# Two weight buffers moved to other start addresses in a TensorE-bound float32r kernel

## The reference

```
first block, 2 layers:
  mod = silu(c) @ w_mod + b_mod                      # shifts, scales, gates
  p = (rms_norm(x) * (1 + scale) + shift) @ w_in
  mix = [attention, fourier, conv, pool](p) @ w_out
  x = x + gate1 * mix
  x = x + gate2 * ((silu(xn @ w_a) * (xn @ w_g)) @ w_ffn_out)
second block, 2 layers:
  layer 0: retention and a short convolution, gated, @ w_out
  layer 1: low-rank (latent) causal attention, gated, @ w_out
  h = h + rms_norm(y) * post_norm
```

## Time and profile before

| | |
|---|---|
| median of 3 runs | 2270.41 us (2269.43 to 2270.57) |
| time of the profiled execution | 2271.93 us |
| its span from first to last instruction | 2269.8 us |
| TensorE matmul busy | 2203.6 us, 97% |
| TensorE weight load busy | 1776.2 us, 78% |
| VectorE busy | 1176.1 us, 52% |
| ScalarE busy | 732.7 us, 32% |
| GpSimd busy | 633.6 us, 28% |
| mean granted TensorE clock | 0.986 |

### The profile page before, as it was taken

The page is one execution under the profiler, slowest core; times in us unless marked ns, Lnnn a source line. Parts: engine busy times, 40 slices in busy tenths (PEclk is TensorE's granted clock), DMA queues, the critical chain, the costliest instruction groups (busy, mean ns, idle before and its releaser), DMA issues.

```text
span 2269.8 us, 26814 instructions
## 1 busy us (share of the span) xinstructions
PE 2203.6 (97%) x11148; PEld 1776.2 (78%) x11148; DVE 1176.1 (52%) x1533; ACT 732.7 (32%) x1101; POOL 633.6 (28%) x272
## 2 busy tenths in 40 slices
PE   8998899999999999999999999999999999999998
PEld 6874587888888888785678888887778888888756
DVE  6987577666555665686455213246332344442172
ACT  4333424121112121424542212223263222334652
POOL 0000003223332233200144444433223444323402
PEclk9999999999999999999999999999999999989999
DMA  8312241333333342211023323323222333311301
GB/s 315 108 37 84 75 148 61 117 130 129 103 112 130 118 145 82 70 56 75 19 87 95 117 78 95 117 76 93 77 64 93 93 99 96 93 54 55 106 14 56
DMA packets 59592, 214.14 MB, mean 94 GB/s; under 512 B 6608, under 2 KB 10320, under 8 KB 58320
## 3 DMA queue, kind: packets, MB, share of 16 engines
q1 hardware_dynamic: 57024, 206.57, 27.8%
q10 hardware_dynamic: 2448, 5.85, 0.8%
HBM read 210.30 MB, written 2.10 MB: 94 GB/s over the span
## 4 chain that ended last, share of the span: by engine, by line
PE 89%; DVE 6%; ACT 3%; issue 1%; POOL 1%; DMA 0%; POOLq 0%; ACTq 0%; DVEq 0%
PE prod L592 74%; PE misc L638 1%; PE prod L727 1%; PE prod L807 1%; PE prod L775 1%; PE prod L862 1%; PE misc L1038 1%; PE misc L714 1%; DVE conv_acc L1941 1%; PE prod L691 1%; DVE stat L1872 1%; PE misc L886 1%; PE misc L682 1%; PE misc L874 1%; PE misc L648 1%
## 5 line engine op out<-in xcount | busy, mean ns | idle before, releaser
L571 POOL TENSOR_TENSOR wlo<-ring,whi 128x1024 fp32r<-128x1024 f32 (+3 forms) x252 | 601.9, 2389 | 1581.6 <-ACT whi L1132 1581.6
L592 PE MATMUL prod<-operand_hi,whi 128*128 128x512 f32 (+1 forms) x2080 | 682.8, 370 | 11.2 <-POOL operand_lo L558 5.5
L592 PE MATMUL prod<-operand_lo,whi 128*128 128x512 f32 (+1 forms) x2080 | 674.0, 365 | 0.0
L592 PE MATMUL prod<-operand_hi,wlo 128*128 128x512 f32 (+1 forms) x2080 | 670.6, 364 | 0.0
L1132 ACT ACTIVATE whi<-ring 128x1024 fp32r<-128x1024 f32 (+3 forms) x278 | 287.3, 1034 | 712.6 <-PE prod L592 691.2
L592 PEld LDWEIGHTS prod<-operand_hi,whi 128*128 128x128 f32 x2080 | 353.8, 188 | 88.7 <-issue 9.6
L592 PEld LDWEIGHTS prod<-operand_hi,wlo 128*128 128x128 f32 x2080 | 355.4, 188 | 66.7
L592 PEld LDWEIGHTS prod<-operand_lo,whi 128*128 128x128 f32 x2080 | 354.5, 188 | 63.1 <-issue 2.2
L592 PE MATMUL prod<-hidden_lo,whi 128*128 128x512 f32 (+1 forms) x528 | 160.8, 359 | 0.0
L592 PE MATMUL prod<-hidden_hi,whi 128*128 128x512 f32 (+1 forms) x528 | 159.0, 355 | 0.0
L592 PE MATMUL prod<-hidden_hi,wlo 128*128 128x512 f32 (+1 forms) x528 | 158.9, 355 | 0.0
(11 more groups left out here) (316 smaller groups left out, 2412.2 us busy)
## 6 DMA issues: line engine op xcount, KB each, us to landing
ring<-in_w SPq DMA_DIRECT2D x224, 512.0 KB, 3.6
modw<-in_wmod SPq DMA_DIRECT2D x68, 512.0 KB, 3.7
ring<-in_w SPq DMA_DIRECT2D x32, 704.0 KB, 4.9
mod_pair<-in_wpair SPq DMA_DIRECT2D x8, 1024.0 KB, 16.8
ring<-in_wmod SPq DMA_DIRECT2D x12, 512.0 KB, 4.4
dft<-in_dftx SPq DMA_DIRECT2D x8, 512.0 KB, 5.4
resid<-in_xt SPq DMA_DIRECT2D x4, 768.0 KB, 7.6
ring<-in_w SPq DMA_DIRECT2D x12, 192.0 KB, 2.3
```

What stands on the lines that cost most here:

```text
L571: nc.gpsimd.tensor_tensor(wlo_of(j)[:, 0:w], ring[PLACE["panel", j] % RING][:, 0:w], whi_of(j)[:, 0:w].bitcast(F32), ALU.subtract).then_in ...
L592: mm = pe.matmul(G[b][:, t0:t0 + tn], w[:, k * P:(k + 1) * P], a[:, t0:t0 + tn], start=(i == 0 and q == 0), stop=(i == g.kc - 1 and q == 2))
```

## The change

The two `wlo` buffers are no longer placed right behind `whi`. 256 bytes are left free ahead of the first, and 64 ahead of the second.

```
         whi = [sb(f"whi{s}", FH * P, F32R) for s in range(2)]
-        wlo = [sb(f"wlo{s}", FH * P, F32R) for s in range(2)]
+
+        top[0] += 256
+        wlo0 = sb("wlo0", FH * P, F32R)
+        top[0] += 64
+        wlo = [wlo0, sb("wlo1", FH * P, F32R)]
```

## The result

The changed kernel takes 2282.45 us in the median of 10 runs, the one before 2270.49 (10 runs): 12.0 us slower by the medians. The ratio of the two is 1.0056 with a 95% interval of 1.0036 to 1.0076. One run of a later kernel, 2739.21 us at a mean granted clock of 0.747, was in a slow state and is left out. The forecast was 2256.6. The rival "Slower" had 2283, with a chance of 0.26.

What follows compares the result with a forecast made beforehand. TensorE's stream of loads and matmuls was taken to bound the kernel. Gains of 10.3 us in mixed and 3.5 in narrow steps, 13.8 together, gave 2270.4 - 13.8 = 2256.6 us; likeliest case 2246 to 2266, wider range beyond 2237 and 2283.

Steps and rivals of the forecast that it cites:

- Slower: Rival, dense streams of line 592: shifted loads stop the stream longer; 7.8 us narrow plus 4.6 mixed, time 2283, chance 0.26.
- what bounds the kernel: TensorE, busy 97% of the span, loses 13.6 ns per narrow matmul and 100.5 ns per mixed step inside its stream.
- the parts costed at nothing: Moves of `par`, `con`, `cosT`, `sinT` and `region`: no cost; new write places for wlo's writers: nothing, some 2 us in the range.
- My value: Main estimate between the bounds: 528 mixed steps of the long piece gain 19.5 ns each, 10.3 us; 13.8 us with narrow steps.
- The second term: Narrow steps: the wlo load gets the same 24% relief, 2.5 ns in each of 1396 steps, 3.5 us gained.
- What would show it: Signs in the profile after: long piece about 549 us, 1152-matmul piece about 260.5; only the matmul beside wlo's load gets shorter.
- No effect: Rival, dense stream: each fast load costs a fixed toll at any place; time 2270, chance 0.19.
- The formula that the prediction took: For TensorE matmuls, N/2.4 + 2.5: 512 columns take some 216 ns, which the float32r trace exceeds by 11 ns.

## Why the prediction was wrong

The prediction's reading of what bounds the kernel held: the time moved by what TensorE loses inside the dense stream, and that loss depends on places below 512 bytes. So did the parts costed at nothing. The moved constants, tables and `region` gave a ratio of 0.9995 alone, the writers of wlo were as fast as before, and the waits for wlo did not grow.

The step that failed is "My value": "New places for a third of the loads upset the slower pattern; I take it that the 528 steps of the long piece ... fall to 1041". The 10.3 us of that term measured 0 in the two profiled executions: the long piece took 558.90 us before and after. Over all executions the term has the other sign: with the odd panels displaced in the mixed stages alone the kernel was 0.21% slower (0.01 to 0.40%), 4.0 us in the mean. That the same step can have two paces in the same places was read rightly, and the runs bear it out for the whole piece (with all places equal within 256 bytes in layer 0, 548.4 in two kernels and 558.9 in three). But it was evidence that the pace follows from the history of the stream, and I used it as evidence for the sign of a change of place. It has none. With displaced parts mixed steps took from 1042 to 1067 ns. (The 528 steps themselves are right, but not by missing records: the trace has all 8604 matmuls of the line, and the first step lies ahead of the piece.)

The second term, a relief of 2.5 ns for a narrow step's load of wlo, had the wrong sign. Narrow steps already ran at the best of all paces seen: with loaded and streamed blocks at equal places within 256 bytes 226.7 ns, and at each of the other distances tried 229.4 to 233.1. I had assumed that beginning at equal places is a collision. The row that spoke against it was in my hands, the fall from 232.5 to 226.9 ns after a pause, and I gave it to the rival only. Nor is the effect confined to the matmul under which `wlo` is loaded, as "What would show it" had it: there it is 2 to 3 ns, and 9 under the next one.

That rival had the mechanism and the place for the narrow steps: a displaced load takes away the stable pace of the dense stream. That its time, 2283, came within 1 us of the measured one is luck in both terms. For the narrow steps it took 5.6 ns in every one of 1396, 7.8 us. Measured, a step at 320 bytes loses 12.8 ns and one at 256 nothing that lasts: 698 steps (half of 1396) times 12.8 are 8.9 us, as an estimate from the panels, and the 12 ns of each even panel add some 1.0. The run with only these panels displaced was 0.32% slower (0.11 to 0.53%), 7.0 us in the mean. For the mixed steps it took a third of the way from 1060.5 to 1080 ns, 4.6 us. Measured were 0.21%, 4.0 us in the mean, and they don't come from a slower long piece in the profiled executions (558.90, 558.71): in the first of these kernels the displaced panels took 8.48 us, as before, and in the second 8.43, though that piece began at a granted clock of 0.57.

What the runs show is that the kernel with odd panels displaced in layer 0 has no executions in the lower of before's two groups, and the changed kernel none under 2276 us. That this is the loss of the 1040 ns pace is not shown directly, since no second execution of the changed kernel was profiled, but three things speak for it. The groups lie some 10 us apart, like the long piece in its two paces (10.5). The five profiles with equal places in layer 0 agree: 548.4 us in executions of 2257.41 us and of 2267.09, each the shortest of its kernel, and 558.9 in those of 2271.93, 2271.92 and 2273.11. And the piece of five panels ahead of the long one, 43.46 us before and 44.06 after, took 43.4 to 43.5 us in four of the five kernels with equal places there (44.1 in the fifth) and 43.6 to 44.4 in all twelve with displaced ones.

"No effect" as a fixed toll at any place is refuted for the part above 226.7 ns. It may hold for the 13.4 ns between 213.3 and 226.7, which no placement took away. As to the rule of the Trainium skill ("TensorE: Matmul & The Clock Gate", section "Step-by-step: what each phase is for") that loading the next weights takes no read bandwidth from the running matmul: the rows disagree. With high and low weights both 64 bytes from the streamed rows the narrow matmul takes 232.9 ns, and with all of them moved by the same 64 bytes it takes 226.67. The formula that the prediction took from the section "Back-to-back issue gap" of the same page of the Trainium skill is given there for an isolated matmul; for a stream of loads and matmuls 512 wide the section has about 131 ns. No row here comes near that: the best pace is 226.67 ns.

Open remain why equal places give the stable pace (that the memory is interleaved within 256 bytes and load and stream keep out of each other's way in step is a guess), what decides between the two paces of the mixed steps, and why the loss has the size that it has at each distance.

## What to carry to other kernels

In a dense stream of float32r matmuls with a weight load each, put everything that TensorE loads and streams at the same place within 256 bytes; here every other distance tried cost 1 to 3% per narrow matmul. Before moving such a buffer, look whether the stream already sits in a pace that repeats to the nanosecond: 226.67 ns is exactly 544 cycles of 2.4 GHz. In this kernel such a locked pace was the best state and not a collision. And where one execution of a kernel may differ from the next by 20 us, compare pieces of the chain, and not single times; with many runs, set the times beside their granted clocks before you compare medians, because two groups can hide behind one median.

## What the runs showed of the hardware that was not expected

- The time of a float32r matmul 512 wide depends on the distance, within 256 bytes, between the block of weights loaded and the rows streamed: 226.67 ns at distance 0 and 256, 229.4 to 233.1 elsewhere; moving both by 64 bytes changes nothing.
- The loss is not a sum over displaced loads: one of three costs 4.2 ns per matmul at 64 bytes, two 5.5, three 6.2. At 192 bytes one costs 4.7, two 3.7 and three 2.7.
- Mixed steps (512 and 256 wide) settle in one of several paces and keep it for over 500 steps. With equal places these were 1060 or 1040 ns, 10.5 us over the piece. Both occur in one execution of the kernel before, at different stages; that the long piece itself changes its pace between executions of one placement is argued from the two groups of times.
